# Gathering a pack's tokens feature-major in one step of 24 products, in a two-layer decoder step

## The reference

```python
def hier_moe(h, w_group, w_router, w_gate_up, w_down):      # 4 groups x 8 experts, top-1 group, top-2 within it
    ...
        gate = jnp.sum(jax.nn.one_hot(eidx, N_EXPERTS, dtype=jnp.float32) * wts[..., None], axis=1)
        gu = jnp.einsum('td,edf->tef', hs, w_gate_up)                       # 1024 -> 2 x 256 per expert
        act = jax.nn.silu(gu[..., :EXPERT_FF]) * gu[..., EXPERT_FF:] * gate[..., None].astype(hs.dtype)
        return jnp.einsum('tef,efd->td', act, w_down)                       # 256 -> 1024
```

## Time and profile before

| | |
|---|---|
| median of 3 runs | 1395.16 us (1389.37 to 1397.46) |
| profiled execution, its own time | 1394.41 us |
| its span, first to last instruction | 1392.5 us |
| TensorE busy | 1249.5 us, 90% of the span |
| VectorE, ScalarE busy | 356.7 us, 153.4 us |
| mean granted TensorE clock | 0.958 of full speed |
| moved by DMA | 365.58 MB, mean 263 GB/s |

### The profile page before, as it was taken

How to read it: one execution, slowest core, us unless ns; L and a number is a source line. 1 busy time by engine, 2 the same in 40 slices (tenths; PEclk the granted TensorE clock), 3 DMA queues, 4 the chain that set the end, 5 groups by cost and what they waited for, 6 DMA issues and landing times.

```text
span 1392.5 us, 13848 instructions
## 1 busy us (share of the span) xinstructions
PE 1249.5 (90%) x5986; PEld 747.2 (54%) x5986; DVE 356.7 (26%) x859; ACT 153.4 (11%) x344; POOL 43.3 (3%) x59
## 2 busy tenths in 40 slices
PE   6999998989979898859999999999899979888775
PEld 3477776766324343337676776454567753332223
DVE  2122113013122222321223132335500042232224
ACT  2000002012101010121111201000200021010001
POOL 0000000000000000000000000223000000000000
PEclk9999999998999999979999999999999969999987
DMA  9643348631799999973233323578984517999992
GB/s 400 271 152 121 128 162 340 259 144 63 289 429 409 426 426 428 428 334 112 85 121 120 137 77 121 196 302 335 368 350 159 181 61 315 427 427 427 428 427 117
DMA packets 27536, 365.58 MB, mean 263 GB/s; under 512 B 3168, under 2 KB 3184, under 8 KB 5328
## 3 DMA queue, kind: packets, MB, share of 16 engines
q1 hardware_dynamic: 23904, 338.92, 60.6%
q10 hardware_dynamic: 1696, 18.88, 3.2%
q0 software_dynamic: 1872, 6.86, 1.2%
HBM read 340.32 MB, written 24.32 MB: 262 GB/s over the span
## 4 chain that ended last, share of the span: by engine, by line
PE 70%; DMA 23%; DVE 3%; ACT 2%; issue 1%; POOL 0%; DVEq 0%; SPq 0%; POOLq 0%; ACTq 0%
PE bank L617 25%; DMA ring<-in_gu 22%; PE bank L425 11%; PE bank L327 8%; PE bank L484 4%; PE bank L757 4%; PE bank L474 2%; PE bank L515 2%; PE bank L312 1%; DMA arena<-out_mk 1%; PE bank L744 1%; PE bank L440 1%; PE bank L348 1%; PE bank L381 1%; PE bank L493 1%
## 5 line engine op out<-in xcount | busy, mean ns | idle before, releaser
L617 PE MATMUL bank<-hT,ring 128*128 128x288 f32 x1408 | 346.3, 409 | 6.3 <-DVE arena L1349 3.2
L617 PEld LDWEIGHTS bank<-hT,ring 128*128 128x128 f32 x1408 | 268.6, 191 | 84.5 <-issue 4.8
L484 PE MATMUL bank<-ring,arena 128*32 128x512 f32 x1024 | 132.1, 652 | 59.4 <-DMA ring<-in_gu 57.7
L425 PE MATMUL bank<-arena,ring 128*128 128x288 f32 x640 | 157.3, 406 | 1.8 <-DVEq L1061 1.8
L425 PEld LDWEIGHTS bank<-arena,ring 128*128 128x128 f32 x640 | 121.4, 190 | 35.6 <-issue 2.2
L327 PE MATMUL bank<-ring,arena 128*128 128x512 f32 x256 | 111.2, 593 | 3.1 <-DVE arena L997 3.1
L484 PEld LDWEIGHTS bank<-ring,arena 128*32 128x32 f32 x1024 | 32.3, 115 | 150.1 <-DMA ring<-in_gu 84.5
L474 PE MATMUL bank<-arena 128*128 128x512 f32 (+1 forms) x192 | 101.5, 656 | 2.2 <-DVE arena L1126 1.5
L327 PEld LDWEIGHTS bank<-ring,arena 128*128 128x128 f32 x256 | 48.2, 190 | 63.4 <-issue 61.9
L474 PEld LDWEIGHTS bank<-arena 128*128 128x128 f32 (+1 forms) x192 | 32.9, 198 | 74.0 <-issue 72.5
L515 PE MATMUL bank<-arena 128*128 128x288 f32 x256 | 69.8, 419 | 2.1 <-issue 1.7
(11 more groups left out here) (199 smaller groups left out, 817.6 us busy)
## 6 DMA issues: line engine op xcount, KB each, us to landing
ring<-in_gu SPq DMA_DIRECT2D x64, 2048.0 KB, 24.7
ring<-in_dn SPq DMA_DIRECT2D x32, 2048.0 KB, 17.8
ring<-in_rin SPq DMA_DIRECT2D x14, 2048.0 KB, 9.0
ring<-in_wkv SPq DMA_DIRECT2D x8, 2048.0 KB, 18.3
ring<-in_cin SPq DMA_DIRECT2D x8, 2048.0 KB, 9.3
ring<-in_kc SPq DMA_DIRECT2D x8, 2048.0 KB, 8.2
ring<-in_vc SPq DMA_DIRECT2D x8, 2048.0 KB, 11.7
ring<-in_st SPq DMA_DIRECT2D x8, 2048.0 KB, 8.7
```

Source lines behind the costliest of these rows:

```text
L425: mm = pe.matmul(bank[1 + o % 4][:, 0:T], w[:, k, :], cat[:, k, :], start=(k == 0), stop=(k == kt - 1))
L484: mm = pe.matmul(bank[2][32 * e:32 * e + 32, :], xt[:, k, 32 * e:32 * e + 32], wv[:, e, kk, :], start=(k == 0), stop=(k == KD - 1), skip_g ...
L617: mm = pe.matmul(outs[o], w[:, o, k, :], src[:, k, :], start=(k == 0), stop=(k == KD - 1))
```

## The change

`pick` now makes `xgT`'s contents at once. For each of the 8 feature blocks and each of the 3 token blocks, the block of `htok` (128 or 32 tokens by 128 features) is stationary and the one-hot (128 slots) moves. The result is features by slots, accumulated over the token blocks in banks 0 and 1, and `x_picked` counts twice a pack, once a bank. `turn_x`, the slot-major copy `xg` and its two copies are gone; ScalarE and VectorE copy banks 0 and 1 straight to `xgT` where they used to copy to `xg`.

```diff
                 def pick(i):
                     pe.wait_ge(S("selected"), PACKS * L + i + 1)
-                    picked(onehot_m, bank).then_inc(S("x_picked"), 1)
-
-                def turn_x(i):
-                    pe.wait_ge(S("xg_out_a"), PACKS * L + i + 1)
-                    turn_picked(0, xg).then_inc(S("xg_turned"), 1)
-                    pe.wait_ge(S("xg_out_d"), PACKS * L + i + 1)
-                    turn_picked(1, xg).then_inc(S("xg_turned"), 1)
+                    for k in range(KD):
+                        for b, (t0, n) in enumerate(BLK):
+                            mm = pe.matmul(bank[k // 4][:, (k % 4) * P:(k % 4 + 1) * P],
+                                           htok[b][0:n, k * P:(k + 1) * P], onehot_m[0:n, b, :],
+                                           start=(b == 0), stop=(b == 2), skip_group_check=True)
+                        if k % 4 == 3:
+                            mm.then_inc(S("x_picked"), 1)
...
                 pick(0)
-                turn_x(0)
...
                     if i:
                         combine(i - 1)
-                    if i + 1 < PACKS:
-                        turn_x(i + 1)
...
                 def picked_out(i):
-                    act.wait_ge(S("x_picked"), PACKS * L + i + 1)
-                    act.activation(xg[:, 0:512], bank[0][:, :], ACT.Copy).then_inc(S("xg_out_a"), 1)
-
-                def turned_out(i):
-                    act.wait_ge(S("xg_turned"), 2 * PACKS * L + 2 * i + 1)
+                    act.wait_ge(S("x_picked"), 2 * PACKS * L + 2 * i + 1)
                     act.activation(xgT[:, 0:4, :], v3(bank[0][:, :], 4), ACT.Copy).then_inc(S("xt_out_a"), 1)
...
                 def picked_out(i):
-                    dve.wait_ge(S("x_picked"), PACKS * L + i + 1)
-                    dve.tensor_copy(xg[:, 512:1024], bank[1][:, :]).then_inc(S("xg_out_d"), 1)
-
-                def turned_out(i):
-                    dve.wait_ge(S("xg_turned"), 2 * PACKS * L + 2 * i + 2)
+                    dve.wait_ge(S("x_picked"), 2 * PACKS * L + 2 * i + 2)
                     dve.tensor_copy(xgT[:, 4:8, :], v3(bank[1][:, :], 4)).then_inc(S("xt_out_d"), 1)
```

More of the change, by code:

```diff
@@ L880, in picked_out @@
                 def picked_out(i):
-                    act.wait_ge(S("x_picked"), PACKS * L + i + 1)
-                    act.activation(xg[:, 0:512], bank[0][:, :], ACT.Copy).then_inc(S("xg_out_a"), 1)
-                def turned_out(i):
-                    act.wait_ge(S("xg_turned"), 2 * PACKS * L + 2 * i + 1)
+                    act.wait_ge(S("x_picked"), 2 * PACKS * L + 2 * i + 1)
                     act.activation(xgT[:, 0:4, :], v3(bank[0][:, :], 4), ACT.Copy).then_inc(S("xt_out_a"), 1)
                 picked_out(0)
-                turned_out(0)
                 for i in range(PACKS):
@@ L900, in experts @@
                     act.activation(GT, bank[7][:, 0:T], ACT.Copy).then_inc(S("gt_out"), 1)
-                    if i + 1 < PACKS:
-                        turned_out(i + 1)
                     act.wait_ge(S("y_sum"), 2 * PACKS * L + 2 * i + 1)
```

## The result

| | before | after |
|---|---|---|
| median, first comparison (5 runs each) | 1395.16 us | 1406.40 us (1397.70 to 1408.75) |
| ratio | | 1.0091, 95% interval 1.0066 to 1.0116 |
| the same kernel again (12 runs, beside 32 of before) | 1391.79 us | 1402.84 us, ratio 1.0075, 1.0047 to 1.0102 |
| profiled execution, its own time | 1394.41 us | 1397.70 us |
| its span | 1392.5 us | 1395.9 us |

The change makes the kernel slower, by 11 us in either comparison. The forecast was 1400.9 us with a range of 1388.5 to 1408.5. The time lies in the range, but the forecast's likeliest outcome, within 0.5% of no change, did not come.

A forecast was written before the change was run, and what follows sets the result against it. Expert loads at 428 GB/s were taken to bound the kernel, TensorE counting only where loads wait for it. Terms 0.7 + 3.4 + 2.4 = +6.5 us on 1394.41 gave 1400.9 us, range 1388.5 to 1408.5.

The forecast's parts named there:

- The cost of the pick: Each pick on TensorE: 24 short products plus 16 changes of stationary height at 0.195 us, 8.5 us against 5.93.
- Layer 0's start: Pick to gate_up at full clock: longer pick, transposes and a copy gone, 9.3 us against 8.61, +0.7 us.
- Layer 1's start: First pick of layer 1 wholly at the lower clock, 14.5 us against 10.4, shorter steps behind it: +2.4 us.
- Rival C: Layer 1's first pick: the clock rises as it did before; total 1397.1 to 1398.5 us, chance 0.20.
- The value packs: Layer 0's two packs with value blocks: DMA already dry, down product 1.7 us later in each, +3.4 us.
- rival B: New pick keeps the clock low in a value pack, 6.3 us more; 1407.2 us for one, 1413.5 both; chance 0.20.
- The other packs: 12 of the 14 picks inside the loop: the extra TensorE time is hidden by 7 us of slack, costing nothing.
- Rival A: Every pick: height changes hidden behind short products, pick 5.3 us; sum -6.1 us, 1388.3 us, chance 0.13.

The follow-up runs named there:

- grouped: The changed kernel with token block outer and feature block inner, two changes of height a pick instead of 16; 1385.23 us, sums wrong.
- padded: The changed kernel with the third token block taken with all 128 rows in every pick, so no change of height; 1381.53 us.
- l1_start_padded: The changed kernel with the third token block at all 128 rows only in the pick of layer 1's pack 0; 1394.75 us.
- filled: The changed kernel with every pick at 128 rows, without changes of height, but 39 products instead of 24; 1391.35 us.
- loop_only: The kernel before with the new pick only for packs 1 to 7 of each layer, pack 0 gathered as before; 1400.73 us.
- value_filled: The changed kernel with 39-product picks without changes of height in layer 0's two value packs alone; 1399.01 us.
- old_padded: The kernel before with its own 6-product pick, the third token block taken with all 128 rows; 1388.83 us.

## Why the prediction came out as it did

**The cost of the pick: right.** 8.5 us was forecast, 8.44 measured. At the lower clock 14.5 for the start; measured 15.03 by the records, of which 0.2 us is the end of the last one (0.42 us long, where the next would follow after 0.21), and a change costs 0.29 us and not 0.28. The choice between 5.3 and 8.5 us rested on the two heights in the earlier trace rows, and the grouped and padded kernels confirm it. "Mode switching requires drain" (the Trainium skill, "TensorEngine Tiling (Array Packing)", Key Properties) fits this, if the two heights are two modes: it holds here for products of 128 columns as for those of 512, and 0.2 us is what each change cost.

**Layer 0's start: right.** 9.3 us and +0.7; measured 9.34 and +0.73. **Layer 1's start: right in place, size and reason** in the profile: the low clock throughout, +2.4 forecast, 15.86 - 13.01 = +2.85 measured, and gate_up behind it took 0.3 us more (8.82 against 8.5), which the sum left out. Rival C did not occur in any of the six profiles with this pick at layer 1's start. In the medians the two starts gave only 1.5, and why is open.

**The value packs: the step that failed.** The term of 1.7 us each, at full clock, was right: 31.79 us from pick to the next gate_up, against 30.15 in the second pack before, +1.64. What was mis-sized is rival B, taken at 0.20 and at 6.3 us. It occurred in 2 of the 8 value packs that were profiled with the stalling pick in its place, and cost 8.7 us each time: the low clock lasts 20 us in one and 27 in the other, outlasts the pick and slows the first of the value products too (16.11 us instead of 13.95 in the profile of l1_start_padded). Two in eight is 4.4 us a launch, and the measured 11 exceed the sum's 6.5 by 4.5. That the medians' excess is just this is argued, from 8 value packs and the clocks of the 17 executions, and the agreement is partly luck: the starts gave 1.6 less than their term, and the packs of the next paragraph gave something. The padded and filled kernels and the pair of picks above show that it is the stalls and not the pick's length that keep the clock down. The prediction argued from the router's stretch in the earlier trace rows that a busy engine need not lift the clock, and used it for layer 1's start only; a value pack's pick often begins at the lower clock too, as the 6.20 us in the earlier trace rows had shown, and the same argument held there. Its condition, that the clock is low as the pick begins, was too wide, though: 14 of 19 such picks rose.

**The other packs: nearly right.** A low pick there cost 0.4 to 1.7 us in the three cases seen (one profile each of loop_only, l1_start_padded and value_filled), where "the slack takes it" put it at nothing. In loop_only the gate_up that ends the wait starts at 1208.26 us before the low pick and at 1268.19 two packs on, 59.9 us, against 58.8 in the changed kernel (1214.50 to 1273.26); a difference of a microsecond between two single executions is a rough figure.

**Rival A** described not the change but the kernel that mends it. Its sum, 6.1 us below before, was short of the padded kernel's 10.3, because it left layer 1's pick at 10.3 us throughout; without stalls it took 7.71 us, and gate_up behind it 7.1 instead of 8.5.

**The profiled execution.** It came out only 3.3 us above before's, less than the sum. In before's value packs the last chunk of gate_up had run at the lower clock both times (3.31 and 3.54 us in place of 1.92), in the changed one's it had not: 3.0 us. Such luck moves a single execution by several us; the medians decide.

## What to carry to other kernels

Where a loop mixes full and partial blocks of the summed dimension, count how often the stationary operand's height changes, and put one price on each change (0.2 us here). Multiplying zeros in the missing rows was cheaper than changing the height. And stalls on TensorE can cost more than their time where the clock has just fallen: here products without stalls brought it back and products with them, in the same place, did not. Ask of every stretch on the critical path whether the engine streams, not only how long it takes.

## What the runs showed that was not expected

- The kernel whose pick streams for 8.8 us in each of 16 packs is as fast as the kernel before (1391.35 against 1391.17 us); the one whose pick has stalls and lasts 8.4 us is 11 us slower.
- From the same low level in layer 1's start, the clock rose 4.4 to 6.1 us into a pick without changes (4.4 in padded, 5.7 in filled and old_padded, 6.1 in l1_start_padded), 5.6 us into the one with 2 changes (grouped, where it fell once more), 9.1 and 9.0 us into the old one with 4 (before, loop_only), and not at all in the one with 16 (six profiles).
- Four sums interleaved in the same partitions of one bank (the grouped order) did not add up (relative error 0.21). "PSUM — Partial Sum Buffer" of the Trainium skill says that two accumulation groups open at once in the same bank and quadrant cannot both use the first-product flag, which fits; no run here takes it apart further.
